# A two-block transformer kernel on Trainium2: constants and x are loaded ahead of the two memories, and taken ahead of them

## What is computed

```python
def rmsnorm(x, g):
    y = x * lax.rsqrt(jnp.mean(x * x, axis=-1, keepdims=True) + EPS)
    return y * g

def first_block(x, mem, ...):
    x = x + 0.5 * swiglu(rmsnorm(x, ffn1_norm), ffn1_wg, ffn1_wu, ffn1_wd)
    h = rmsnorm(x, mix_norm)
    aq, ak, av, bq, bk, bv, cq = split(h @ w_in)
    o_a = diff_attention(rope(rmsnorm(aq)), rope(rmsnorm(ak)), av, ...)
    o_b = chunk_band_attention(rmsnorm(bq), rmsnorm(bk), bv, b_rel_bias)
    mk, mv = split(rmsnorm(mem, mem_norm) @ w_mem_kv)
    o_c = memory_attention(rmsnorm(cq), rmsnorm(mk), mv)
    x = x + merge(o_a, o_b, o_c, sigmoid(h @ w_gate + b_gate)) @ w_out
    x = x + 0.5 * swiglu(rmsnorm(x, ffn2_norm), ffn2_wg, ffn2_wu, ffn2_wd)
    return rmsnorm(x, final_norm)

def second_block(x, mem_2, ...):
    u = rms_norm(x, g_mix)
    ...
    y_x = cross_attention(q_x, mem_2, g_mem, w_mem_kv_2, w_xo)
    ...
    h = x + merge(y_nsa, y_rnn, y_x) @ w_o
    h = h + square(relu(rms_norm(h, g_mlp) @ w_up)) @ w_down
    return rms_norm(h, g_final)
```

## Time and profile before

| | us |
|---|---|
| timed runs, median of 3 | 2541.95 |
| lowest and highest of them | 2539.68, 2542.16 |
| span of the profiled execution, first to last instruction | 2541.5 |
| PE busy in it | 2356.6 (93%) |
| DVE, ACT, POOL busy in it | 1176.9, 979.0, 116.2 |
| PE's first instruction, first product of stage mk | 16.8, 41.8 |

### The profile page before, as it was taken

How to read it: one execution, slowest core, us unless ns; L and a number is a source line. 1 busy time by engine, 2 the same in 40 slices (tenths; PEclk the granted TensorE clock), 3 DMA queues, 4 the chain that set the end, 5 groups by cost and what they waited for, 6 DMA issues and landing times.

```text
span 2541.5 us, 29884 instructions
## 1 busy us (share of the span) xinstructions
PE 2356.6 (93%) x10984; PEld 1863.9 (73%) x10984; DVE 1176.9 (46%) x2183; ACT 979.0 (39%) x1636; POOL 116.2 (5%) x126
## 2 busy tenths in 40 slices
PE   5999999878877999899999899988999998999997
PEld 4788888666655887788888687766666686788886
DVE  4433333665455345433333536553888543532432
ACT  4432223354455433233223433523767433321321
POOL 1000001000000000100001210000000001000000
PEclk8899999889998999899999899999999999999998
DMA  4332323221200333222332372222000132233231
GB/s 179 106 99 80 102 93 89 91 67 38 71 9 26 99 99 116 67 84 86 112 99 68 97 228 80 67 71 82 1 1 2 51 105 81 80 99 99 83 99 50
DMA packets 213465, 206.72 MB, mean 81 GB/s; under 512 B 4832, under 2 KB 194400, under 8 KB 213120
## 3 DMA queue, kind: packets, MB, share of 16 engines
q1 hardware_dynamic: 210368, 192.31, 24.5%
q0 software_dynamic: 3008, 13.24, 1.7%
HBM read 199.25 MB, written 4.19 MB: 80 GB/s over the span
## 4 chain that ended last, share of the span: by engine, by line
PE 86%; DVE 6%; ACT 3%; issue 2%; DMA 1%; POOL 0%; SPq 0%; DVEq 0%; ACTq 0%; POOLq 0%
PE ps L896 25%; PE ps L898 24%; PE ps L897 24%; PE ps L715 4%; PE ps L1049 2%; PE ps L730 2%; ACT whi L603 1%; DVE Sm L847 1%; DMA wraw<-in_w_in 1%; DVE wlo L610 1%; PE ps L1084 1%; PE ps L1041 1%; DMA xin<-in_x 1%; PE ps L1109 0%; DVE Sm L882 0%
## 5 line engine op out<-in xcount | busy, mean ns | idle before, releaser
L610 DVE TENSOR_TENSOR wlo<-wraw,whi 128x2048 fp32r<-128x2048 f32 x192 | 444.1, 2313 | 620.3 <-ACT whi L603 620.3
L896 PE MATMUL ps<-hH,whi 128*128 128x512 f32 x1656 | 651.7, 394 | 19.9 <-DVE hL L1640 17.7
L897 PE MATMUL ps<-hL,whi 128*128 128x512 f32 x1656 | 649.5, 392 | 0.0
L898 PE MATMUL ps<-hH,wlo 128*128 128x512 f32 x1656 | 649.0, 392 | 0.0
L603 ACT ACTIVATE whi<-wraw 128x2048 fp32r<-128x2048 f32 x192 | 366.8, 1910 | 332.3 <-PE ps L898 304.0
L896 PEld LDWEIGHTS ps<-hH,whi 128*128 128x128 f32 x1656 | 313.8, 189 | 94.9 <-issue 27.8
L897 PEld LDWEIGHTS ps<-hL,whi 128*128 128x128 f32 x1656 | 313.9, 190 | 66.0 <-issue 0.2
L898 PEld LDWEIGHTS ps<-hH,wlo 128*128 128x128 f32 x1656 | 313.4, 189 | 66.6
L896 PE MATMUL ps<-gH,whi 128*128 128x512 f32 x608 | 239.8, 394 | 0.0
L898 PE MATMUL ps<-gH,wlo 128*128 128x512 f32 x608 | 239.6, 394 | 0.0
L897 PE MATMUL ps<-gL,whi 128*128 128x512 f32 x608 | 239.6, 394 | 0.0
(11 more groups left out here) (323 smaller groups left out, 2469.9 us busy)
## 6 DMA issues: line engine op xcount, KB each, us to landing
wraw<-in_w_in SPq DMA_DIRECT2D x45, 1024.0 KB, 5.2
wraw<-in_ffn_wg SPq DMA_DIRECT2D x22, 1024.0 KB, 5.3
wraw<-in_ffn_wu SPq DMA_DIRECT2D x22, 1024.0 KB, 5.3
wraw<-in_w_up SPq DMA_DIRECT2D x16, 1024.0 KB, 5.6
wraw<-in_w_down SPq DMA_DIRECT2D x16, 1024.0 KB, 5.5
wraw<-in_ffn_wd SPq DMA_DIRECT2D x16, 768.0 KB, 4.8
wraw<-in_w_gate SPq DMA_DIRECT2D x12, 1024.0 KB, 5.1
wraw<-in_ffn_wd SPq DMA_DIRECT2D x16, 640.0 KB, 4.4
```

The lines of the kernel that those rows point to most:

```text
L610: dve.tensor_tensor(wlo[s][:, :], wraw[s][:, :], f32(whi[s][:, :]), ALU.subtract).then_inc(w_lo[s], 1)
L896: pe.matmul(o, lh, rh, start=start, stop=False)
L897: pe.matmul(o, lh, rl, start=False, stop=False)
L898: return pe.matmul(o, ll, rh, start=False, stop=stop)
```

## The change

On SyncE's queue `cst` goes first, then both halves of x, then `vec`, then the two memories. On ScalarE the wait for `cst` and `vec` and the eight squares of x stand ahead of the work on the memories. On VectorE the eight copies of x stand ahead of the scaling of the memories. TensorE's and GpSimd's streams are as before. Code that isn't moved stands one line higher up (a number lower by one) behind the loads.

```diff
         @block.sync
         def _(sp):
-            for m, name in enumerate(("mem", "mem_2")):
-                sp.dma_start(memx[m][:, :, :], a[name][0].rearrange("(m p) d -> p m d", p=P)).then_inc(mem_in[m], 16)
-                if m == 0:
-                    sp.dma_start(cst[:, :], a["cst"]).then_inc(cst_in, 16)
-                    sp.dma_start(vec[:, :], a["vec"]).then_inc(cst_in, 16)
+            sp.dma_start(cst[:, :], a["cst"]).then_inc(cst_in, 16)
             for h in range(2):
                 sp.dma_start(xin[:, 2 * h:2 * h + 2, :],
                              a["x"][0].rearrange("(m p) d -> p m d", p=P)[:, 2 * h:2 * h + 2, :]).then_inc(x_in, 16)
+            sp.dma_start(vec[:, :], a["vec"]).then_inc(cst_in, 16)
+            for m, name in enumerate(("mem", "mem_2")):
+                sp.dma_start(memx[m][:, :, :], a[name][0].rearrange("(m p) d -> p m d", p=P)).then_inc(mem_in[m], 16)
...
             act.wait_ge(pool_cst, 4)
             order = Order(act, act_step)
+            act.wait_ge(cst_in, 32)
+            for c in range(DC):
+                act.wait_ge(xt_ready, c + 1)
+                act_sq(act, 0, c)
             for m in range(2):
                 act.wait_ge(mem_in[m], 16)
                 for t in range(MT):
                     order(act.activation(prod_junk[:, 0:D], memx[m][:, t, :], ACT.Square, accum_out=st[:, 64 + 2 * m + t:65 + 2 * m + t]))
                 act.activation(st[:, 68 + 2 * m:70 + 2 * m], st[:, 64 + 2 * m:66 + 2 * m], ACT.Sqrt, bias=eps[:, 0:1], scale=1.0 / D).then_inc(mem_sd, 1)
-            act.wait_ge(cst_in, 32)
-            for c in range(DC):
-                act.wait_ge(xt_ready, c + 1)
-                act_sq(act, 0, c)
...
+            for c in range(DC):
+                dve.wait_ge(x_turned, c + 1)
+                dve.tensor_copy(xT[:, c, :], ps[6 + c % 2][:, :]).then_inc(xt_ready, 1)
             for m in range(2):
                 dve.wait_ge(mem_sd, m + 1)
                 order(dve.reciprocal(st[:, 72 + 2 * m:74 + 2 * m], st[:, 68 + 2 * m:70 + 2 * m]))
                 for t in range(MT):
                     ins = dve.tensor_scalar(memx[m][:, t, :], memx[m][:, t, :], st[:, 72 + 2 * m + t:73 + 2 * m + t], None, ALU.mult)
                 ins.then_inc(mem_norm_ready, 1)
-            for c in range(DC):
-                dve.wait_ge(x_turned, c + 1)
-                dve.tensor_copy(xT[:, c, :], ps[6 + c % 2][:, :]).then_inc(xt_ready, 1)
```

## The result

| | before | changed |
|---|---|---|
| median, us | 2539.74 | 2544.44 |
| lowest to highest, 20 runs each | 2537.15 to 2542.49 | 2540.04 to 2545.8 |
| ratio of the times, 95% interval | | 1.0017 (1.001 to 1.0024) |
| span of the first profile | 2541.5 | 2543.6 |
| first product of mk | 41.76 | 44.12 |

The changed kernel takes 0.17% more, inside the 0.2% that was set as the bound of no change: the likeliest case of the prediction, and its sign. The prediction's 2544.7 lies close to 2544.44, but by luck. It was built on a median of three runs, 2541.95; twenty runs of the same kernel gave 2539.74. The difference that was forecast, 2.7 us, has to be held against 2540 x 0.0017 = 4.3 us (2.5 to 6.1). A starting point that was 2.2 us too high made up for a difference that was too small.

The account below looks back on a forecast made before the run. TensorE, busy 93% of the span, bounds the kernel, so only its first product's start, set by the prologue's waits, matters. Terms -5.15 + 1.28 + 6.59 = +2.7 us on 2541.95 gave 2544.7 us (+0.11%), range 2541.0 to 2548.0.

Parts of the forecast that it names:

- the likeliest case: Whole kernel: time within 0.2% of before, counted as no change, on the slow side; chance 0.88.
- x lands earlier, -5.15: Loads in the prologue: x complete at 11.53 in place of 16.68 us; bounds -4.6 to -5.4.
- The table load, +1.28: ScalarE before the first square of x: the load, hidden before, goes on the path; bounds 0 to 1.28 us.
- that rival: ScalarE: a pause of about 1.3 us behind each table load on the path, time 2546.0 us; chance 0.05.
- The squares' pace, unchanged: ScalarE and GpSimd: first square to start of `whi` stays about 10.3 us, from 14.84 to 25.1.
- The memories' work, +6.59: ScalarE between squares and `whi`: work formerly hidden goes on the path, `whi` at 31.7 us; bounds 6.4 to 6.8.
- Sum: Prologue: -5.15 + 1.28 + 6.59 = +2.7 us, first product at about 44.5; bounds +1.0 to +3.9.
- The median of the runs lies 0.45 above that span: Whole kernel: links the profiled span, 2541.5 to 2544.2 us, with the timed median, 2541.95 + 2.7 = 2544.7.
- the clock, taken as 0: TensorE around mk: some 8 slow products cost 1.6 us; the change may give -1.6 to +1.6.
- The slow rival: TensorE at mk: starts at 1.2 GHz and stays longer; 16 more slow products give 2547.9 us; chance 0.10.
- The faster rival: Prologue: memories' work stays hidden, so the earlier x pays, 2538.1 or 2536.8 us; chance 0.05.
- the one on the order of landing: Loads: evenly shared bandwidth keeps x near 16.7 us, sum +7.9, time 2549.8 us; chance 0.02.

Follow-up runs that it names:

- takers alone: Kernel before with its old loads, but squares and copies of x ahead of the memories on ScalarE and VectorE: 2549.89 us, ratio 1.0033.
- early Sqrt: Changed kernel plus one single-column Sqrt ahead of ScalarE's first wait, so the table loads early: 2541.22 us, ratio 1.0007 to the kernel before.
- that with the squares last: Changed kernel plus a single-column Sqrt ahead of ScalarE's first wait and the squares of x moved behind mH: 2534.85 us, ratio 0.9976 to the kernel before.
- woven run: Changed kernel plus a first Sqrt, squares of x between ScalarE's other work, first product waiting for eight mL, not sixteen: 2533.32 us, ratio 0.9965 to before.
- filled run: Changed kernel plus unread identity transposes in TensorE's two idle stretches before mk: 2543.41 us, ratio 1.0014 to the kernel before.
- its three sets: Changed kernel timed three times without further edit: 2544.44, 2545.07 and 2544.71 us, ratios 1.0017, 1.0019 and 1.0017 to the kernel before.
- second label: Kernel before run again without edit under a label of its own: 2541.78 us, ratio 1.0007 to the kernel before.

## Why the prediction was right, and what of it was not

Step by step, at the first product, where the profiles repeat to 0.1 us:

- *x lands earlier, -5.15.* TensorE started at 11.43 against 16.82: -5.39, the end of the bounds. VectorE's work on `vec` ended as the first turned chunk was there, as said.
- *The table load, +1.28.* First square 14.72 against 18.71, -3.99 = -5.39 + 1.40. Confirmed by its removal (1.3 to 1.4 at the first product). No pause of its own followed a load: 13.43 + 1.28 = 14.71, next at 14.72. The drain that the Trainium skill gives in "ScalarE: Activation LUTs", section "What ACT_TABLE_LOAD costs", stays unseen, and that rival falls: two loads taken away gave 2.5 us.
- *The squares' pace, unchanged.* 14.72 to 24.98 against 18.71 to 28.99: 10.26 and 10.28.
- *The memories' work, +6.59.* 24.98 to 31.35: 6.37, since each operation starts a little before the one ahead of it ends.
- *Sum.* +2.7 forecast, +2.4 found at the first product; 2.36, 2.44 and 2.34 us between profiles at the feed-forward part where the clock went the same way (90.56 to 88.22, 88.50 to 86.06).

What was off is the step from the profile to the runs. "The median of the runs lies 0.45 above that span" sets two different executions side by side. In the runs since, the device time of an execution is 1.75 to 2.3 us over its own span, 1.8 in most. The first profile of before was then an execution of some 2543.3, slow for its kernel (its clock was low in a stretch where that of the second profile was high). The 0.45 drops out of the forecast, which is 2541.95 + 2.7. Its two parts were off in opposite directions: the median of three was 2.2 us above that of twenty, and the 2.7 was 1.6 us under the measured 4.3. If that surplus is real, it could in this sum only lie in the clock, taken as 0 with 1.6 us on either side; no term of the prologue has room for it, since the first product came 0.3 us sooner than the sum said.

The slow rival (mk begins on a cold array, that is at the low clock) was half right. It did begin so in one of three profiles of the changed kernel, with 13 products at the low level, and the feed-forward part came 3.5 us later behind the first product than with none; the other two had 8 and none, as the two of the kernel before had. The one profile each of the takers alone, of the early Sqrt, of that with the squares last and of the woven run began low too. Whether the change makes the cold start more frequent is not shown. The rule of the Trainium skill's "TensorE: Matmul & The Clock Gate", section "Part 4: PE-mode transpose", that transposes don't bring the full clock, isn't borne out: in the earlier trace rows and in the filled run the clock rose during transposes alone. The faster rival and the one on the order of landing fell: x was there at 11.4.

**What stays open.** Whether the 4.3 us measured is more than the 2.4 us of the prologue. The three ratios say so weakly (the lower ends are 2.0 to 2.5 us). A clock that is low for more products on average when mk starts at 44.1 would do it, and two of three profiles of the changed kernel had a low stretch, against one of two before; that is too few to tell. The mean granted clocks of the timed runs don't decide it. They are lower in the changed kernel (0.9623 to 0.9628 on average in its three sets, against 0.9640 to 0.9647 in those of the kernel before). But its profiles have TensorE at the low level for 17 to 22 us ahead of the first product, against 10 us before, as it now stands idle between x and the first memory; that costs no time and makes up 0.0014 to 0.0022 by itself. Against a surplus speaks that the kernel before, under its second label, has a median 2.3 us above that of the same kernel's thirty runs beside it.

## What to carry to other kernels

Moving loads earlier is worth only what the engines can then take in that order: here the wait for x had been the cover of 6.4 us of ScalarE's work and of a table load, and the change spent the 5.4 us that it won on uncovering both. Before reordering loads, look for what else stands in an in-order engine between the landing and its use; the larger win (7 us) lay in moving eight squares, whose sum is used at 80 us, out of the way of the weights. Judge a change of a microsecond or two by the start of a fixed instruction, not by the span of one profile.

## What the hardware showed that was not expected

- ScalarE's table for Sqrt served Square and Copy as well: with Sqrt used first, one load was left in the prologue where a first Square had needed two.
- The same program, with its first product within 0.1 us, ran that stage at 17 or at 10 products in 3.4 us from one execution to the next, by the granted clock alone (1.00 or 0.5). Spans of one kernel differed by 6.4 us (2541.5 and 2535.1).
- GpSimd's sum of 128 x 512 and VectorE's subtraction of 128 x 2048 hold each other up when they meet: 2.83 and 3.20 us in place of 1.27 for the two sums, and 3.36 in place of 2.29 for the second of the two subtractions. The woven run reads as if they took turns (an inference from start and end times): the first subtraction kept its 2.29 us and ended at 24.32, the sum issued at 22.61 ended 1.12 us behind that, the second subtraction 2.16 us behind the sum, and the next sum 1.12 us behind that again. Beside VectorE's copies from PSUM the sums kept their 1.26 to 1.28 us. The Trainium skill's "GPSIMD Engine Reference", section "1. Specifications", names such a contention with VectorE instructions that have two SBUF inputs; this trace agrees.
- During the first transposes, at 11.4 as at 16.8 us, TensorE took 0.21 us from one to the next though the profile gives a clock of 1.00 there, and 0.11 us later in the same stretch (the first memory's at 23.8 us). At 36.3 us, where the profile gives 0.50, it is 0.21 too. That the array was at the low level in both, and the record wrong ahead of its first change, is the likely reading; it isn't shown by itself.
